# A gated linear recurrence kernel: masked scores no longer added on VectorE, one product of scores and values per direction

## The reference

```python
def gla_forward(q, k, v, log_f, s0):
    ...
    s_prev, _ = _inter_chunk_states(k_c, v_c, b_c, s0)
    o_inter = jnp.einsum('bhnck,bhnkv->bhncv', q_c * jnp.exp(b_c), s_prev)
    a = jnp.einsum('bhnck,bhnsk->bhncs', q_c * jnp.exp(b_c - b_mid), k_c * jnp.exp(b_mid - b_c))
    a = jnp.where(jnp.tril(jnp.ones((CHUNK, CHUNK), dtype=bool)), a, 0.0)
    o_intra = jnp.einsum('bhncs,bhnsv->bhncv', a, v_c)
    return (o_inter + o_intra).reshape(b, h, t, -1)

# in hgrn2_mixer
o_f = gla_forward(q, k_f, v, lf_f, s0_f)
o_b = _rev(gla_forward(_rev(q), _rev(k_b), _rev(v), _rev(lf_b), s0_b))
o = (o_f + o_b)
```

## Time and profile before

| | |
|---|---|
| median of 3 runs | 2186.71 us (2184.49 to 2187.04) |
| the profiled execution | 2185.45 us, its span 2183.6 us |
| PE busy | 2059.5 us, 94% |
| DVE busy | 1317.0 us, 60% |
| ACT busy | 920.6 us, 42% |
| POOL busy | 495.3 us, 23% |
| granted TensorE clock, mean | 0.991 |
| first head (step 0 to the end of step 22) | about 62 to 258 us |
| each further head | 164 us, the last ends at about 1403 us |

### The profile page before, as it was taken

How to read it: one execution, slowest core, us unless ns; L and a number is a source line. 1 busy time by engine, 2 the same in 40 slices (tenths; PEclk the granted TensorE clock), 3 DMA queues, 4 the chain that set the end, 5 groups by cost and what they waited for, 6 DMA issues and landing times.

```text
span 2183.6 us, 30077 instructions
## 1 busy us (share of the span) xinstructions
PE 2059.5 (94%) x11372; PEld 1489.0 (68%) x11554; DVE 1317.0 (60%) x2360; ACT 920.6 (42%) x1960; POOL 495.3 (23%) x450
## 2 busy tenths in 40 slices
PE   5789999999999999999999999899999999999998
PEld 2567767767767767767767767677766666666665
DVE  7847647647647647647647647855564537465444
ACT  5735445445445445445445445444422131314222
POOL 2022222222222222222222222210052313100000
PEclk8999999999999999999999999999999999999999
DMA  7220120120120120120120120443321111104443
GB/s 274 81 64 11 35 63 11 34 63 11 35 63 11 35 63 11 35 63 11 35 63 11 35 63 1 144 156 134 117 80 54 39 53 39 64 29 141 147 150 117
DMA packets 106752, 144.45 MB, mean 66 GB/s; under 512 B 7136, under 2 KB 74224, under 8 KB 105584
## 3 DMA queue, kind: packets, MB, share of 16 engines
q1 hardware_dynamic: 99648, 125.72, 18.1%
q10 hardware_dynamic: 6960, 16.80, 2.0%
HBM read 108.91 MB, written 33.57 MB: 65 GB/s over the span
## 4 chain that ended last, share of the span: by engine, by line
PE 76%; DVE 9%; ACT 7%; issue 5%; DMA 1%; POOL 0%; SPq 0%; DVEq 0%; ACTq 0%; POOLq 0%
PE bank L1311 21%; PE bank L1312 21%; PE bank L1316 19%; PE bank L1467 3%; PE bank L1446 3%; PE bank L1551 3%; PE bank L1478 2%; PE bank L1453 1%; DVE w_st L1120 1%; ACT kp L756 1%; DVE xa L1084 1%; PE bank L1430 1%; DMA ada_sb<-in_ada_w 1%; DVE lacc L1150 1%; DVE xb L1037 1%
## 5 line engine op out<-in xcount | busy, mean ns | idle before, releaser
L1311 PE MATMUL bank<-h_hi,w_hi 128*128 128x512 f32 (+1 forms) x1472 | 575.9, 396 | 0.0
L1312 PE MATMUL bank<-h_hi,w_lo 128*128 128x512 f32 (+1 forms) x1472 | 549.7, 378 | 0.0
L1311 PEld LDWEIGHTS bank<-h_hi,w_hi 128*128 128x128 f32 x1472 | 278.9, 190 | 54.9
L1312 PEld LDWEIGHTS bank<-h_hi,w_lo 128*128 128x128 f32 x1472 | 279.0, 190 | 47.6
L1316 PE MATMUL bank<-h_lo,w_bf 128*128 128x512 bf16 (+1 forms) x1351 | 303.2, 364 | 8.0 <-issue 1.3
L1316 PEld LDWEIGHTS bank<-h_lo,w_bf 128*128 128x128 bf16 x1472 | 133.8, 98 | 142.7 <-issue 25.1
L1120 DVE SCALAR_TENSOR_TENSOR w_st<-w_st,cv,bank 128x128 f32<-128x128 f32 x560 | 193.7, 346 | 23.7
L612 POOL TENSOR_TENSOR q<-qp,cv 128x512 f32<-128x512 f32 x64 | 79.9, 1249 | 536.9 <-DVE qp L1065 226.2
L1311 PE MATMUL bank<-wo_hi,og_hi 128*128 128x512 f32 x496 | 197.7, 399 | 3.1 <-DVE og_lo L1157 2.2
L1312 PE MATMUL bank<-wo_hi,og_lo 128*128 128x512 f32 x496 | 193.5, 390 | 0.0
L586 POOL TENSOR_TENSOR w_hi<-w_raw,zero_col 128x512 fp32r<-128x512 f32 x80 | 92.8, 1160 | 432.2 <-DMA w_raw<-in_w_in 229.9
(11 more groups left out here) (180 smaller groups left out, 3628.4 us busy)
## 6 DMA issues: line engine op xcount, KB each, us to landing
w_raw<-in_w_in SPq DMA_DIRECT2D x80, 256.0 KB, 2.7
ada_sb<-in_ada_w SPq DMA_DIRECT2D x8, 1024.0 KB, 14.1
xt<-in_x SPq DMA_DIRECT2D x16, 512.0 KB, 6.7
ada_a<-in_ada_late SPq DMA_DIRECT2D x64, 128.0 KB, 2.1
ada_b<-in_ada_late SPq DMA_DIRECT2D x64, 128.0 KB, 2.2
gated_scratch<-o_t ACTq DMA_DIRECT2D x32, 256.0 KB, 2.4
xr<-in_x SPq DMA_DIRECT2D x16, 512.0 KB, 4.9
x_scratch<-xr ACTq DMA_DIRECT2D x16, 512.0 KB, 2.6
```

The source lines that it names most:

```text
L1311: pe.matmul(out_ap, hi, m_hi, start=start, stop=False)
L1312: pe.matmul(out_ap, lo, m_hi, start=False, stop=False)
```

## The change

Forward and backward are now alike. TensorE multiplies the masked scores of its own direction with the values right behind the state products of each block, in both directions (four more products for each of the four forward blocks of a head). VectorE's addition is gone. `am` has the same four buffers, but two for each direction, used by turns; `am_b` and `asum` are gone. The freed memory holds `lacc` and the `ada1` buffers, which share nothing any more with `k_tok` and `am`. With that, the waits for the late part are gone from SP, ScalarE and GpSimd, and the late work has other steps: in the first head two pieces a step at steps 4 to 12 and sums at steps 11 and 14 (before: 9 and 10), in the others pieces as before and sums at steps 8 and 12 (before: 7 and 10). In the last head the late vector goes out one step earlier (LATE_OUT 18 instead of 19).

```diff
-def late_pieces(st, first, top):
-
-    if first:
-        n = 4 if st == 9 else 3
-        seen = range(3 * (st - 5), 3 * (st - 5) + n) if 5 <= st <= 9 else range(0)
-        return seen[:1] if top else seen[1:]
-    i = 2 * (st - 1) - (1 if top else 0)
-    return range(i, i + 1) if 0 <= i < NLATE else range(0)
+def late_index(st, first, top):
+
+    i = 2 * (st - (4 if first else 1)) - (1 if top else 0)
+    return i if 0 <= i < NLATE else None
...
-    return {9: 0, 10: 1}.get(st) if first else {7: 0, 10: 1}.get(st)
+    return {11: 0, 14: 1}.get(st) if first else {8: 0, 12: 1}.get(st)
...
-LATE_OUT = 19
+LATE_OUT = 18
...
-                    for top in (False, True):
-                        for i in late_pieces(st + top, first, top):
-                            if i == 0 and first:
-                                sp.wait_ge(s["hf_ready"], KT * len(GT0))
-                            if i == 0:
-                                need(sp, "u_done", NF, h, 0)
+                    for i in (late_index(st, first, False), late_index(st + 1, first, True)):
+                        if i is not None:
                             load_late(h, i)
...
-            pool.wait_ge(s["gate_out"], 16)
...
-                        if fi == 0:
-                            need(act, "late_acc", NLATE, h, NLATE)
-                        if fi == 1:
-                            need(act, "late_mm", 2, h, 2)
...
-                    if 6 <= fi < NF:
-                        ai = lat(fi)
-                        need(dve, "a_masked", NA, h, ai + 1)
-                        need(dve, "o_done", NA, h, ai)
-                        dve.tensor_tensor(asum[:, :, :], am[:, GROUPS[F0 + fi][1], :, :], am_b[:, :, :], ALU.add
-                                          ).then_inc(s["a_summed"], 1)
...
-                        if d == 1:
-                            need(dve, "a_summed", 4, h, ai - 4)
-                        dve.copy_predicated(am[:, ai, :, :] if d == 0 else am_b[:, :, :],
+                        dve.copy_predicated(am[:, 2 * d + ai % 2, :, :],
...
-                            last = pe.matmul(o[r, c // 2 * P:(c // 2 + 1) * P],
-                                             q2[:, ai % 2, c * CHUNK:(c + 1) * CHUNK],
-                                             w_st[:, (8 * ai + n) % 16, :], start=(n < 2), stop=(d == 0),
+                            pe.matmul(o[r, c // 2 * P:(c // 2 + 1) * P], q2[:, ai % 2, c * CHUNK:(c + 1) * CHUNK],
+                                      w_st[:, (8 * ai + n) % 16, :], start=(n < 2), stop=False,
+                                      skip_group_check=True)
+                        need(pe, "a_masked", NA, h, ai + 1)
+                        for j in range(4):
+                            last = pe.matmul(o[:, j * P:(j + 1) * P], am[:, 2 * d + ai % 2, j, :],
+                                             v_tok[:, 2 + 4 * b + j, :], start=False, stop=True,
                                              skip_group_check=True)
-                        if d == 1:
-                            need(pe, "a_summed", 4, h, ai - 3)
-                            for j in range(4):
-                                last = pe.matmul(o[:, j * P:(j + 1) * P], asum[:, j, :], v_tok[:, 2 + 4 * b + j, :],
-                                                 start=False, stop=True, skip_group_check=True)
```

More of the change, by code:

```diff
@@ L168, in hybrid_kernel @@
         extra_at = cursor[0]
-        asum = place("asum", [P, 4, P], FP32)
-        junkh = place("junkh", [P, 2, P], BF16)
-        hss = place("hss", [P, 4], FP32)
-        hrs = place("hrs", [P, 4], FP32)
-        em = place("em", [P, 8], FP32)
-        cv = place("cv", [P, NF, 8], FP32)
-        assert cursor[0] <= extra_at + 6 * P * 4
+        lacc = place("lacc", [P, 2, LCOL], FP32)
+        ada1_b = place("ada1_b", [P, LCOL], FP32)
         cursor[0] = extra_at + 6 * P * 4
@@ L186, in hybrid_kernel @@
         q2 = place("q2", [P, 2, BLK], FP32)
-        k_tok_at = cursor[0]
         k_tok = place("k_tok", [P, 2, 4, P], FP32)
@@ L191, in hybrid_kernel @@
         start_end = cursor[0]
+        junkh = place("junkh", [P, 2, P], BF16)
+        hss = place("hss", [P, 4], FP32)
+        hrs = place("hrs", [P, 4], FP32)
+        em = place("em", [P, 8], FP32)
         ge = place("ge", [P, NF, 9], FP32)
-        am_b = place("am_b", [P, 4, P], FP32)
-        cursor[0] = k_tok_at
-        ada1 = (place("ada1_a", [P, LCOL], FP32), place("ada1_b", [P, LCOL], FP32))
-        lacc = place("lacc", [P, 2, LCOL], FP32)
-        cursor[0] = after_h
+        cv = place("cv", [P, NF, 8], FP32)
+        late_at = cursor[0]
+        ada1_a = place("ada1_a", [P, LCOL], FP32)
+        ada1 = (ada1_a, ada1_b)
+        late_end = cursor[0]
+        cursor[0] = late_at
         grow = place("grow", [4 * KT, P], FP32)
+        assert cursor[0] <= late_end
         cursor[0] = kp_at
@@ L997, in head @@
                     if first and st == F0:
-                        dve.wait_ge(s["zero_done"], 5)
-                    late_piece(h, late_pieces(st, first, True))
+                        dve.wait_ge(s["zero_done"], 4)
+                    late_piece(h, late_index(st, first, True))
                     if st == LATE_ADD:
@@ L1136, in head, with late_piece @@
                         gate_out(h, st - (F0 + 11))
-                    late_piece(h, late_pieces(st, first, False))
-            def late_piece(h, pieces):
-                for i in pieces:
-                    k, half = i % KT, i // KT
-                    need(dve, f"late_in{i % 2}", 8 * NLATE, h, 16 * (i // 2 + 1))
-                    if k == 0:
-                        need(dve, "late_mm", 2, h, half - 1)
-                        dve.tensor_scalar(lacc[:, half, :], ada1[i % 2][:, :], head_tab[:, k, 4:5], None, ALU.mult
-                                          ).then_inc(s["late_acc"], 1)
-                    else:
-                        need(dve, "late_acc", NLATE, h, i)
-                        dve.scalar_tensor_tensor(lacc[:, half, :], ada1[i % 2][:, :], head_tab[:, k, 4:5],
-                                                 lacc[:, half, :], ALU.mult, ALU.add).then_inc(s["late_acc"], 1)
+                    late_piece(h, late_index(st, first, False))
+            def late_piece(h, i):
+                if i is None:
+                    return
+                k = i % KT
+                need(dve, f"late_in{i % 2}", 8 * NLATE, h, 16 * (i // 2 + 1))
+                if k == 0:
+                    need(dve, "late_mm", 2, h, i // KT - 1)
+                    dve.tensor_scalar(lacc[:, i // KT, :], ada1[i % 2][:, :], head_tab[:, k, 4:5], None, ALU.mult
+                                      ).then_inc(s["late_acc"], 1)
+                else:
+                    need(dve, "late_acc", NLATE, h, i)
+                    dve.scalar_tensor_tensor(lacc[:, i // KT, :], ada1[i % 2][:, :], head_tab[:, k, 4:5], lacc[:, i // KT, :],
+                                             ALU.mult, ALU.add).then_inc(s["late_acc"], 1)
             def rest_tile(layer, i):
```

3 lines of the change are left out of this document (1 added, 2 removed).

## The result

The changed kernel takes 2175.24 us, median of five runs (2174.30 to 2175.61), against 2185.26 us for the kernel before in the same session; the ratio is 0.995 with a 95% interval of 0.9938 to 0.9961. The interval leaves out 1, so the kernel is faster, by 0.5%. The profiled execution spans 2172.6 us, 11.0 less than before.

The account below looks back on a forecast made before the run. TensorE (94% busy) was taken as the bound, with slack only where VectorE and ScalarE pace steps 12 to 20. Heads -3.2 and first head's late part -4.5 gave -7.7 us: 2177.7 from the profile, stated as 2178.8; range 2170 to 2186.

Parts of the forecast that it names:

- The sum: Whole kernel: -3.2 us from the eight heads and -4.5 us from the first head's late part, together -7.7 us.
- costed at nothing: Side effects given 0 us: moved late sums in other heads, SP's earlier loads, GpSimd's gate wait, `grow` a step earlier.
- The forward products: Four fp32 products per forward block of each head: 1.09 us of TensorE a group, 34.9 us for 32.
- That rival: Forward products at the skill page's price, 0.65 us a group instead of 1.09: 2172.4 us, chance 0.04.
- The walk through a head: TensorE's delay carried through steps 14 to 22 of a middle head: next head starts 0.6 us earlier.
- The sums' move: Late sums of the other heads from steps 7 and 10 to 8 and 12: the same TensorE work, 0 us.
- The sum on VectorE: Addition ahead of the chain in steps 18 to 21, 0.59 us; removed, chains are ready 0.6, 1.2 us and more earlier.
- The rival that the lead isn't given back: Steps 20 to 22: something else sets them, so the heads gain nothing; 2183.3 us, chance 0.17.
- the slower one: ScalarE's read at step 17 comes late and its loop follows TensorE: 1.84 us lost a head, 2196.9 us, chance 0.08.
- The late part of the first head: First head, steps 9 to 14: step 10's stall goes, scan of step 12 at 164.2 against 168.73; -4.5 us.
- a wait of the key turn above 2 us: First head, steps 12 and 13: new TensorE waits of this size were named as a sign the prediction was wrong.
- The last head: No weight preparation at steps 19 and 20, so less wait to absorb the delay; ends about 1.1 us later.

Follow-up runs that it names:

- `products_only`: The changed kernel with the late part scheduled as before the change in all heads (pieces and sums); 2182.39 us.
- `sum_back`: The changed kernel with an addition put back on VectorE at steps 18 to 21 of each head, its result unused; 3.9 us more in the median.
- `first_head_old`: The changed kernel with only the first head's late part as before (pieces at steps 5 to 9, sums at 9 and 10); 4.2 us more.
- `first_early`: The changed kernel with the first head's late-part pieces at steps 4 to 8, sums still at 11 and 14; 2175.05 us.
- `best`: The changed kernel with late-part pieces at steps 4 to 8 (first head) and 0 to 8 (others), step 9's weight loads issued at step 7; 2165.53 us.
- `best2`: As `best`, but the first head's sixteen pieces follow VectorE's idle time, spread over steps 3 to 8; 2163.01 us.
- `loads_ahead`: The changed kernel with only the weight loads of step 9 moved to step 7 of SyncE's program; 1.1 us under the changed kernel.
- `sums_7_10`: The changed kernel with the late part's sums at steps 7 and 10, as before, in all heads but the first; median 2.4 us higher.

## Why the prediction was right, and where it was off

**The number.** The sum was -7.7 us, measured are -10.0 in the medians and -11.0 in the spans. (From the median of 2186.71 the sum gives 2179.0; 2178.8 was written.) The time lies inside the range, near its fast side. The signs of the terms and their mechanisms hold. The middle heads are mis-sized, and one thing that was costed at nothing is part of that.

**The forward products.** One group is 1.09 us (386.67 and the next group at 387.76), as the identical group's row said. By the Trainium skill, "TensorE: Matmul & The Clock Gate", section "Back-to-back issue gap", the estimate was 0.65 us; the trace disagrees, and even the second identical group takes 0.89. That rival is out.

**The walk through a head.** The prediction had TensorE late by 1.09, 1.09, 2.18 and 1.84 us at the narrow parts of steps 15, 16, 17 and 18, by 1.21 at step 20, and early by 0.44 at 21 and 0.6 at the end. Measured in the fifth head: 0.98, 0.94, 2.04, 1.60, 0.88, then -0.85 and -0.99. This head is 0.11 us early at step 14 already; from there on it is 1.09, 1.05, 2.15, 1.71, 0.99, then -0.74 and -0.88. The form is right. **This is the mis-sized term of the sum**: -0.6 us a middle head, where the runs show -0.87 for the products and the addition (`products_only`, net) and -1.17 for all.

Where the missing 0.27 lies, the walk shows. The three waits that go wholly (steps 17, 19 and 20) each bring 0.06 to 0.10 us more than their row says. Those of steps 15 and 22, of which something is left, bring what their rows say. Most of the excess can be seen. Before, third head, step 20:

```profile
564.31 0.60 PE L1430 MATMUL bank<-ident,kp 128*128 128x128 f32 x4
566.55 1.09 PE L1446 MATMUL bank<-w_st,q 128*64 128x128 f32 x16 [1.65 <-issue]
```

The turn starts 2.24 us ahead of the state products; after, 0.53 (395.23 and 395.76 above). That is 1.71 us for a wait listed as 1.65: a turn of 0.60 us costs only 0.53 when the next matmul follows at once. What goes beyond that is not explained.

The rest of the 1.17 us is two things. The sums' move, costed at nothing, gives 0.15 us. The wait at step 12 gives another 0.16: it is 0.78 us on average before and 0.62 after, mostly by when a load lands, and that is luck and not the change. It makes 1.0 of the 11 us between the two profiles.

**The sum on VectorE.** By the walk it is worth 0.6 us a head, what VectorE's lead at steps 20 and 22 allows. `sum_back` gives 0.61 net. The rival that the lead isn't given back is out, as is the slower one: ScalarE's read waited at steps 18 and 19, but held nobody.

**The late part of the first head.** -4.5 us predicted, 4.0 to 4.2 measured by undoing it alone. In `products_only` the same undoing costs the first head 5.0 us from step 3 on; there the clock is at 0.50 from 150.0 to 156.8 us, and in `first_head_old` from 146.8 to 153.6. The scan of step 12 was set at 164.2 and stands at 163.71. The second head starts 5.4 us earlier in all, where -4.5 and -0.6 make 5.1. The prediction named a wait of the key turn above 2 us there as a sign that it was wrong, and 2.66 came. The size holds all the same, since it went by VectorE's scan and not by that wait; what it didn't see is that the lower clock comes back for 3 us. That the figure fits so well is in part luck: the scan came 5.0 us earlier (168.73 to 163.71), and what this brought is 4 to 5 us by where the slow stretch falls.

**The last head.** +1.1 predicted, +0.66 measured. The walk itself was right: from step 14 on the head loses 1.05 us. It is 0.39 us early there already, 0.26 by the load wait of step 12 (0.83 before, 0.57 after) and 0.13 by the sums' move.

**Costed at nothing.** The sums' move: 0.15 us a head net, about 1 us in all.

**The layers behind the heads.** From the first matmul of the output projection to the end the profile before takes 778.2 us and the profile after 779.0. It is no effect of the change. Six of the fourteen profiles have 778.0 to 778.3 there (`first_early`, `sum_back`, `best` and `best2` among them, with the changed kernel's code) and the other eight 778.9 to 779.3. What makes the two values stays open.

## What to carry to other kernels

A wait on the bound engine is a budget that can be filled once: 34.9 us of new products cost 6.7, the next 28.5 cost 26.3. Carry the delay from step to step through the list of waits, rather than adding up shares, and add what a restart costs (0.06 to 0.10 us here for each wait that goes wholly). Small work on another engine is priced by where it stands: the same pieces, one step earlier, were worth 8 us, more than the change as a whole gave in the middle heads, since they no longer stood ahead of a clamp and a scan, there beside GpSimd's weight preparation. Before believing a fraction of a microsecond, find the wait that varies from one repetition to the next and take it off. And compare two traces step by step: a figure for a whole head had credited the products with what a late sum's new place gave.

## What the runs showed of the hardware

Four fp32 products of 128x128x128 take 1.09 us as the first group behind other work, and 0.89 us when the same four follow again.

A VectorE addition of two SBUF operands takes 0.67 us alone and 1.75 beside GpSimd's weight preparation; even a clamp with one operand goes from 0.28 us (alone, in `loads_ahead`) to 1.12. The chain, whose second tensor is read from PSUM, takes 3.11 us beside the same work and 3.12 without. The Trainium skill, "SBUF — State Buffer", section "SBUF: two separate sides", gives the shared pair of ports as an exclusive lock between GpSimd and VectorE operations with two SBUF inputs or in a two-port mode. The addition agrees in kind. The clamp has one input and would have to be in a two-port mode, which no trace here shows.

The granted clock has two values in these traces, 0.50 and 1.00; what lies between is a mean over both. Behind a stall of TensorE in the first head it is 0.50 from 150 to 154.5 us behind 5.79 us, 0.50 from 158 to 161 behind 2.66 us, 0.50 from 159.5 to 162.5 behind 2.33 us (`best`), and 1.00 behind 0.65 us (`best2`). Behind the 1.65 us of a middle head before (402.45 to 405.45) it is 1.00. The length of the stall alone doesn't decide. TensorE waits 2.5 us for the first matmul of the output projection in every kernel here. Behind it the clock is at 0.50 in nine of the fourteen profiles and at 1.00 in five; after, then before:

```profile
1393.60:1396.60 3.00, 3.00 (x7) 0.50 0.07 26
1405.40:1408.40 3.00, 3.00 (x13) 1.00 0.07 26
```

It cost nothing there: from that matmul to the first one of the pooling layer both take 191.1 us. In the first head it does cost: `sums_7_10`, with the clock at 0.50 until 163.9 us and not 161.1, loses 1.5 us more than the changed kernel at that place.
